# Expert weights of the first quad: per-expert rows of 4 KB for the later half of k, and one give-back for their four slots

## The chip, the core and the metric

The kernel runs on one core of a Trainium2 chip. The metric is the device time of one execution in microseconds, the median of the runs shown. TensorE (PE) multiplies matrices, VectorE (DVE) and ScalarE (ACT) work elementwise, GpSimd (POOL) does a few odd jobs, and SyncE (SP) issues nearly all DMA transfers: it waits on semaphores and puts one transfer after another on a hardware queue, which 16 DMA engines work off in order.

## What is computed

Two layers of a decoder trunk for 256 tokens of width 1024. Each layer has a token mixer (a wide projection, three branches, an output projection) and then a hierarchical mixture of experts. Only the expert part is touched:

```python
def hier_moe(h, w_rg, w_re, w_gate, w_up, w_down):
    ...
    hg = jnp.einsum("nd,edf->nef", t, w_gate)      # 32 experts, d = 1024, f = 256
    hu = jnp.einsum("nd,edf->nef", t, w_up)
    a = jax.nn.silu(hg) * hu * combine[..., None].astype(t.dtype)
    return jnp.einsum("nef,efd->nd", a, w_down).reshape(b, s, d)
```

Every expert has three matrices of 1 MB in float32 (gate, up, down), so a layer reads 96 MB of expert weights.

## The kernel before

**Tiling.** The 32 experts of a layer are taken in eight quads of four. For a quad, PE gathers the chosen tokens (up to 32 for each expert), multiplies them with gate and up, ACT and DVE make the activation, PE multiplies with down and scatters the result back. The contraction over d is cut into eight steps, k = 0 to 7. A row of a weight matrix in memory, seen from one partition p, holds all eight k of that partition one after another: 8 x 256 floats, 8 KB.

**The ring of weight slots.** Weights arrive in slots of 2048 floats for each partition, 1 MB. A quad needs 12 slots (`QUAD_LOADS`): eight for gate and up, four for down. `pos` numbers the 96 loads of a layer in order; `places(pos)` gives the slot, and 20 slots (`RING_E`) are used in turn, so the load at `pos` goes where `pos - 20` was. Pos 0 and pos 11 have places of their own.

**The first quad** is split by k, so that its slots come free step by step. `FIRST_CHUNKS` says which chunk each of pos 0 to 7 holds: a chunk is one pair of k (`part`, 0 to 3) for one pair of experts (`pair`, 0 or 1), both gate and up. `load_expert` (L482) issues two transfers of 512 KB for it (L489), each of 128 partitions x 2 experts x 512 floats, that is rows of 2 KB. All other expert weights go by L498: one transfer of 1 MB in rows of 8 KB.

**When the loads are issued.** The first 20 loads go out while the token mixer before is still running, in the order of `load_ahead`, as its buffers come free: pos 2 and 3, then pos 4, 5 and 9, pos 6 and 10, pos 8, pos 7, pos 0, 14, 15, pos 1, 18, 19, 20, 12, 16, then 13, 17 and 11. PE waits for the weights of pos 4 to 7 by one group semaphore before the third k pair (`wait_weights(pe, 2 * i, routed)` where i is even).

**When slots are given back.** `quads_sp` (L1981) walks on from pos 21 in strict order. Each load waits until PE has read the slot it will overwrite:

```python
if 0 < pos - RING_E < 6:
    sp.wait_ge(R.gu_part, FIRST_CHUNKS[i] // 2 + 1)
elif pos > RING_E and i < 8:
    sp.wait_ge(R.gu_ready, n + 1)
elif pos > RING_E:
    sp.wait_ge(R.y_ready, 2 * (n + 1))
```

`first_quad` (L2092) runs `gather_pair(i)` and `gate_up_pair(i)` for i = 0 to 3. The first three raise `gu_part`, the fourth raises `gu_ready`. So pos 21 and 22 (down weights of quad 1, experts 1 and 2) go out after the first pair, pos 23 (down, expert 3) after the second, pos 24 and 25 (gate and up of quad 2, expert 0) after the third, pos 26 and 27 (gate and up of quad 2, expert 1) after the fourth. Pos 28 to 30 wait for the end of the first quad's down products (`y_ready`), pos 32 and on for the second quad's gate and up.

The weight lines of PE are L2087 (gate and up, first quad), L2142 (gate and up, quads 1 to 6), L2216 (down) and L2116 (gather).

Of the kernel before, what the change touches and what calls it, by code (L numbers as in the profile page):

```python
# [24 lines left out]
P = 128  # L25
# [20 lines left out]
GROUPS, PER_GROUP, F = 4, 8, 256  # L46
# [32 lines left out]
def trunk_program(nc, x, positions, norm1_g, w_in, b_in, attn_sinks, sgu_ln_g, sgu_ln_b, w_spatial,  # L79
# [4 lines left out]
    TB, KB = S // P, D // P  # L84
    assert TB == 2 and KB == 8 and D_IN == ZG + 3 * D

    with ExitStack() as whole:
# [38 lines left out]
        RING_T, RING_A, RING_E = 4, 12, 20  # L126
# [100 lines left out]
        def places(pos, n=1, routed=False):  # L227

            if pos == HELD and not routed:
                return xs[:].rearrange("p t d -> p (t d)").rearrange("p (s n) -> p s n", s=1)  # L230
            if pos == 0:
                return first_slot[:].rearrange("p (s n) -> p s n", s=1)
            s = PLACES[(pos - 2) % RING_E]
            return arena_slots[:, s:s + n, :] if s < RING_A else rest_slots[:, s - RING_A:s - RING_A + n, :]
# [236 lines left out]

        PART = 2 * F
        SPLIT_LOADS = 8
        FIRST_CHUNKS = (2, 0, 1, 3, 4, 5, 6, 7)

        def first_parts(slot):

            return slot.rearrange("p (e a n) -> p e a n", e=2, a=2)

        LAST_DOWN = LAYER_LOADS - 2  # L480

        def load_expert(sp, l, pos, done, routed=False):  # L482

            slot = places(pos, routed=routed)[:, 0, :]
            if pos < SPLIT_LOADS:
                part, pair = divmod(FIRST_CHUNKS[pos], 2)
                for to, w in enumerate((w_expert_gate, w_expert_up)):
                    src = w[l, 2 * pair:2 * pair + 2].rearrange("e (p k) f -> p e (k f)", p=P)
                    sp.dma_start(first_parts(slot)[:, :, to, :], src[:, :, part * PART:(part + 1) * PART]).then_inc(done, 16)  # L489
                return  # L490
            n, i = divmod(pos, QUAD_LOADS)
            if i < 8 and n == QUADS - 1:
                w, e = (w_expert_gate, w_expert_up)[i // 4], i % 4
            elif i < 8:
                w, e = (w_expert_gate, w_expert_up)[i % 2], i // 2
            else:
                w, e = w_expert_down, i - 8
            sp.dma_start(slot, w[l, 4 * n + e].rearrange("(p k) f -> p (k f)", p=P)).then_inc(done, 16)  # L498
# [139 lines left out]
        def trunk_stage(l):  # L638
            with ExitStack():
# [75 lines left out]
                with ExitStack():  # L715
                    @block.sync
                    def _(sp):
# [54 lines left out]
                        def load_ahead(*slots):  # L772
                            for slot in slots:
                                at = PLACES.index(slot) + 2 if slot != PLACES[-1] else 1
                                at += RING_E if at == HELD else 0
                                load_expert(sp, l, at, arrival(False, at))
# [46 lines left out]
                        load_ahead(3, 7)  # L823
                        sp.wait_ge(merged, 4)
                        load_expert(sp, l, 0, arrival(False, 0))
                        sp.wait_ge(quarter_ready, 12)
                        load_ahead(14, 15)
# [967 lines left out]
        def expert_stage(l):  # L1795
# [4 lines left out]
            def wait_weights(eng, pos, routed):  # L1800

                if routed:
                    eng.wait_ge(again_in[pos % RING_E // 4], landed(0, pos, True))
                else:
                    eng.wait_ge(expert_in[pos % RING_E // 4], landed(l, pos))
                    if pos // 4 in (HELD // 4, (HELD + RING_E) // 4):
                        eng.wait_ge(last_up_in, 48 * (l + 1))
                if pos in SINGLE:
                    eng.wait_ge(arrival(routed, pos), (1 if routed else l + 1) * (16 if pos else 32))
# [163 lines left out]
            def load(sp, pos, routed):  # L1973
                if pos > LAST_DOWN and not routed:
                    return
                if pos > LAST_DOWN - 4 and not routed:
                    load_last_down(sp, l, pos - (LAST_DOWN - 3))
                else:
                    load_expert(sp, l, pos, arrival(routed, pos), routed)

            def quads_sp(sp, R, first, last, routed):  # L1981
                for pos in range(first, last):
                    if pos == HELD + RING_E and not routed:
                        continue
                    n, i = divmod(pos - RING_E, QUAD_LOADS)
                    if 0 < pos - RING_E < 6:
                        sp.wait_ge(R.gu_part, FIRST_CHUNKS[i] // 2 + 1)
                    elif pos > RING_E and i < 8:
                        sp.wait_ge(R.gu_ready, n + 1)
                    elif pos > RING_E:  # L1990
                        sp.wait_ge(R.y_ready, 2 * (n + 1))
                    load(sp, pos, routed)
# [74 lines left out]
            def quads_pe(pe, R, a, b, routed):  # L2067
# [8 lines left out]
                def gate_up_pair(i):  # L2076

                    if i % 2 == 0:
                        wait_weights(pe, 2 * i, routed)
                    for k in (2 * i, 2 * i + 1):  # L2080
                        if k < FIRST_DVE:
                            pe.wait_ge(R.first_dve, k + 1)
                        else:
                            pe.wait_ge(R.first_act, k - FIRST_DVE + 1)
                        for e in range(4):
                            w = first_parts(places(FIRST_CHUNKS.index(2 * i + e // 2))[:, 0, :])[:, e % 2, :, (k % 2) * F:(k % 2 + 1) * F]
                            mm = pe.matmul(ps[e * EC:(e + 1) * EC, 0, :].rearrange("p (a f) -> p a f", a=2),  # L2087
                                           xsel[:, k, e * EC:(e + 1) * EC], w, start=(k == 0), stop=(k == KB - 1),
                                           skip_group_check=True)
                    mm.then_inc(R.gu_part if i < 3 else R.gu_ready, 1)  # L2090
# [335 lines left out]
            def extra_rounds_sp(sp, ahead, at):  # L2426

                with seldom(sp, "sp", ahead) as n_extra:
                    for pos in range(at - RING_E, at, 4):
                        wait_weights(sp, pos, False)  # L2430
                    with sp.Fori(0, n_extra):
                        sp.wait_ge(arrive_a, 3)
                        for s in (ex_ranges[(l + 1) % 2], again_range, arrive_a, go_b, go_c):
                            sp.sem_clear(s)
                        sp.sem_inc(go_a, 1)
                        quads_sp(sp, O, 0, LAYER_LOADS, True)
                        sp.wait_ge(arrive_b, 3)
                        for s in (ex_ranges[(l + 1) % 2], again_range, arrive_b, go_a):
                            sp.sem_clear(s)
                        sp.sem_inc(go_b, 1)  # L2440
                    sp.wait_ge(arrive_c, 3)
                    sp.sem_clear(arrive_c)
                    for pos in range(at - RING_E, at):
                        load_expert(sp, l, pos, reload_in)
                    sp.wait_ge(reload_in, 16 * RING_E)
                    sp.sem_clear(reload_in)
                    sp.sem_inc(go_c, 1)

            @block.sync
            def _(sp):  # L2450
                ahead = sp.mark_branch_hint_location()
                sp.wait_ge(quarter_ready, 18)
                for i in range(RING_E):
                    if PLACES[i] in (13, 17):
                        load(sp, i + 2, False)
                sp.wait_ge(logits_ready, 1)
                sp.wait_ge(squares, 2)
                sp.wait_ge(x_copied, 1)
                load(sp, HELD, False)
                at = CUT * QUAD_LOADS + RING_E  # L2460
                sp.sem_inc(mid, 1)
                quads_sp(sp, E, RING_E + 1, at, False)
                sp.wait_ge(cleared, l + 1)
                extra_rounds_sp(sp, ahead, at)
                quads_sp(sp, E, at, LAYER_LOADS, False)
                if not hands_over:
                    sp.dma_start(gf, norm_f_g.partition_broadcast(P)).then_inc(final_in, 16)
# [147 lines left out]
```

## Time and profile before

| | us |
|---|---|
| three timed runs | 1018.99, 1019.67, 1020.12 |
| median | 1019.67 |
| span of the profiled execution, first to last instruction | 1018.6 |
| PE busy, and its share of the span | 957.3 (94%) |
| main DMA queue, share of 16 engines over the span | 79.6% |

The profiled execution's time outside its span is not listed; the median stands 1.07 us above the span. The page cuts the span in 40 slices of 25.5 us. DMA traffic has two long stretches near its highest rate, in slices 11 to 20 and 31 to 39; slices 13 to 20 and 33 to 39 are the expert stages of the two layers, where it is mostly about 425 GB/s. Layer 1 repeats layer 0 with a shift of some 501.8 us. In the granted clock of TensorE nearly all slices stand at full speed.

### The profile page before, as it was taken

To read this page: it belongs to the slowest core of one execution; us is meant where nothing else is said; L and a number is where in the kernel's file an instruction comes from. 1 tells how busy PE (TensorE), PEld (TensorE's weight loads), DVE (VectorE), ACT (ScalarE), POOL (GpSimd) and SP (SyncE) were. 2 spreads that over 40 slices of the span, in tenths; PEclk is the share of its full clock that TensorE was granted. 3 is DMA by queue.
4 is the path that set the end of the run, shared out by engine and by line. 5 is a ranking of instruction groups with operands and counts; after the bars stand their busy time and mean duration, and the time that the engine had idled before them with its cause. 6 is when DMAs were issued, how large, how long until landed. Compare 5 with 4: busy or idle time off the path is not lost.

```text
span 1018.6 us, 15602 instructions
## 1 busy us (share of the span) xinstructions
PE 957.3 (94%) x5898; PEld 666.4 (65%) x5898; DVE 561.1 (55%) x1328; ACT 431.8 (42%) x920; POOL 58.6 (6%) x74
## 2 busy tenths in 40 slices
PE   9999999999999995987999999999999999978876
PEld 7888877778886441533588888777878954334333
DVE  7666788786883332211276668787869633222212
ACT  5434666766444110210354355676764441111122
POOL 1120400000010000000004004000000100000000
PEclk9999999999999999989999999999999999999999
DMA  9975643247999999999997755332589999999996
GB/s 348 349 244 190 196 134 125 83 127 268 409 361 418 425 427 425 425 426 427 418 399 245 233 185 186 124 124 83 172 304 383 386 425 424 425 424 425 427 428 264
DMA packets 97114, 313.03 MB, mean 307 GB/s; under 512 B 13424, under 2 KB 18576, under 8 KB 74512
## 3 DMA queue, kind: packets, MB, share of 16 engines
q1 hardware_dynamic: 96704, 312.04, 79.6%
q8 instruction: 44, 0.72, 0.3%
q14 instruction: 30, 0.25, 0.1%
q10 hardware_dynamic: 336, 0.02, 0.0%
HBM read 310.20 MB, written 1.84 MB: 306 GB/s over the span
## 4 chain that ended last, share of the span: by engine, by line
PE 76%; DMA 13%; SPq 7%; DVE 2%; ACT 1%; issue 1%; POOL 0%; DVEq 0%; POOLq 0%
PE ps L1478 16%; PE ps L1479 15%; PE ps L1480 15%; SPq L498 6%; PE ps L2142 6%; DMA arena<-in_w_expert_up_dram 5%; DMA arena<-in_w_expert_gate_dram 3%; DMA ring_rest<-in_w_expert_up_dram 3%; DMA ring_rest<-in_w_expert_down_dram 3%; PE ps L2116 2%; PE ps L1601 2%; PE ps L1503 2%; PE ps L2216 2%; PE ps L1613 2%; PE ps L2228 2%; PE ps L2087 1%
## 5 line engine op out<-in xcount | busy, mean ns | idle before, releaser
L1130 DVE TENSOR_TENSOR split_w<-arena,split_w 128x512 fp32r<-128x512 f32 (+1 forms) x352 | 233.1, 701 | 101.7 <-ACT split_w L923 98.3
L1478 PE MATMUL ps<-split_w,split_a 128*128 128x512 f32 (+1 forms) x736 | 284.3, 386 | 0.1
L1480 PE MATMUL ps<-split_w,split_a 128*128 128x512 f32 (+1 forms) x736 | 277.0, 376 | 0.0
L1479 PE MATMUL ps<-split_w,split_a 128*128 128x512 f32 (+1 forms) x736 | 276.9, 376 | 0.0
L923 ACT CAST split_w<-arena 128x1024 fp32r<-128x1024 f32 (+1 forms) x171 | 176.2, 1033 | 177.2 <-PE ps L1480 170.3
L1478 PEld LDWEIGHTS ps<-split_w,split_a 128*128 128x128 f32 x736 | 138.5, 188 | 27.9 <-issue 3.4
L1480 PEld LDWEIGHTS ps<-split_w,split_a 128*128 128x128 f32 x736 | 138.4, 188 | 25.9
L1479 PEld LDWEIGHTS ps<-split_w,split_a 128*128 128x128 f32 x736 | 138.7, 188 | 23.2
L2373 DVE SCALAR_TENSOR_TENSOR acts<-ps,wslot,acts 128x256 f32<-128x256 f32 x16 | 7.7, 484 | 168.6 <-ACT acts L2043 145.3
L2142 PE MATMUL ps<-arena,rows 128*32 128x512 f32 x416 | 92.0, 631 | 8.0 <-DMA arena<-in_w_expert_up_dram 4.6
L2142 PE MATMUL ps<-ring_rest,rows 128*32 128x512 f32 x352 | 77.9, 639 | 9.2 <-DMA arena<-in_w_expert_up_dram 9.2
L2043 ACT ACTIVATE acts<-ps,rslot 128x256 f32<-128x256 f32 x16 | 7.6, 474 | 151.0 <-PE ps L2142 146.2
L2116 PEld LDWEIGHTS ps<-arena,work 128*128 128x128 f32 x448 | 52.7, 196 | 28.7 <-issue 24.6
L2116 PE MATMUL ps<-arena,work 128*128 128x128 f32 x448 | 55.6, 283 | 15.5 <-issue 8.8
L2228 PE MATMUL ps<-rows,st 128*128 128x512 f32 x112 | 55.3, 617 | 0.9 <-DVE xs L2354 0.7
L1006 ACT ACTIVATE probs<-probs,neg 128x128 f32<-128x128 f32 x112 | 49.7, 447 | 10.5 <-DVE neg L1254 10.5
L2216 PE MATMUL ps<-arena,acts 128*32 128x512 f32 x272 | 46.3, 639 | 6.1 <-ACT acts L2047 4.2
L1149 DVE SCALAR_TENSOR_TENSOR arena<-ps,rstd,arena 128x512 f32<-128x512 f32 (+2 forms) x68 | 47.2, 730 | 3.9 <-PE ps L1480 3.7
L2142 PEld LDWEIGHTS ps<-arena,rows 128*32 128x32 f32 x416 | 24.1, 116 | 37.6 <-issue 37.6
L2142 PEld LDWEIGHTS ps<-ring_rest,rows 128*32 128x32 f32 x352 | 20.0, 117 | 38.4 <-issue 38.3
L2357 DVE TENSOR_TENSOR xs<-ps,xs 128x512 f32<-128x512 f32 x48 | 33.2, 692 | 18.2 <-PE ps L2228 18.2
L2390 DVE COPY rows<-ps 128x512 f32<-128x512 f32 x14 | 9.7, 692 | 54.3 <-PE ps L2216 54.3
(284 smaller groups left out, 1084.3 us busy)
## 6 DMA issues: line engine op xcount, KB each, us to landing
arena<-in_w_in_dram SPq DMA_DIRECT2D x62, 1024.0 KB, 5.3
arena<-in_w_expert_down_dram SPq DMA_DIRECT2D x36, 1024.0 KB, 19.8
arena<-in_w_expert_gate_dram SPq DMA_DIRECT2D x34, 1024.0 KB, 24.5
arena<-in_w_expert_up_dram SPq DMA_DIRECT2D x32, 1024.0 KB, 24.2
ring_rest<-in_w_expert_down_dram SPq DMA_DIRECT2D x24, 1024.0 KB, 18.2
ring_rest<-in_w_expert_gate_dram SPq DMA_DIRECT2D x22, 1024.0 KB, 24.2
ring_rest<-in_w_expert_up_dram SPq DMA_DIRECT2D x22, 1024.0 KB, 25.9
arena<-in_w_proj_a_dram SPq DMA_DIRECT2D x8, 1024.0 KB, 4.9
```

The lines of the kernel that those rows point to most:

```text
L498: sp.dma_start(slot, w[l, 4 * n + e].rearrange("(p k) f -> p (k f)", p=P)).then_inc(done, 16)
L923: act.copy(whi[:, jj % 2, 0:2 * w], half_slot(jj, w)).then_inc(hi_ready, 1)
L1006: act.activation(probs[:, i, n, lo:hi], probs[:, i, n, lo:hi], ACT.Exp, bias=neg[:, i, tb, n:n + 1], accum_out=den[:, i, tb, n:n + 1])
L1130: dve.tensor_tensor(wlo[:, jj % 2, cols], half_slot(jj, w)[:, cols], whi[:, jj % 2, cols].bitcast(F32), ALU.subtract).then_inc(low_split i ...
L1149: dve.scalar_tensor_tensor(out=z[:, tb, cols], in0=ps[:, bank + tb, 0:w], scalar=rstd[:, tb:tb + 1], in1=z[:, 0, cols], op0=ALU.mult, op1= ...
L1478: pe.matmul(o, hi, rhs_hi, start=first, stop=False)
L1479: pe.matmul(o, hi, rhs_lo, start=False, stop=False)
L1480: return pe.matmul(o, lo, rhs_hi, start=False, stop=last)
L2116: mm = pe.matmul(ps[:, 4 + k // 4, (k % 4) * QUAD:(k % 4 + 1) * QUAD], work[:, tb, k * P:(k + 1) * P], onehot[:, n % 2, tb, :], start=(tb ...
L2142: mm = pe.matmul(ps[e * EC:(e + 1) * EC, n % 2, :].rearrange("p (a f) -> p a f", a=2), xsel[:, k, e * EC:(e + 1) * EC], w, start=(k == 0), ...
L2216: mm = pe.matmul(ps[e * EC:(e + 1) * EC, 2 + nh, :], at_sb[:, kf, e * EC:(e + 1) * EC], w, start=(kf == 0), stop=(kf == 1), skip_group_che ...
L2228: pe.matmul(ps[:, 4 + tb, :], st[:, n % 2, tb * P:(tb + 1) * P], y[:, nh * BANK:(nh + 1) * BANK], start=True, stop=True).then_inc(R.back_r ...
```

## The change

For pos 4 to 7, which before held the k pairs 2 and 3 as chunks of two experts, each slot now holds one expert: `pos - 4`. The slot has gate for k = 4 to 7 in its first half and up for k = 4 to 7 in its second. Each half is one transfer of 512 KB in rows of 4 KB (128 partitions x 1024 floats). The number of transfers, their bytes, their order on the queue and the semaphores that they raise stay. PE reads the same numbers from the new places: gate and up of one k lie 1024 floats apart where they lay 512 apart. Since each of the four slots is now read in both the third and the fourth k pair, all four are given back by `gu_ready`: pos 24 and 25 wait for the fourth pair instead of the third. Pos 21 to 23 keep their waits, and pos 26 and 27 too.

```diff
-        FIRST_CHUNKS = (2, 0, 1, 3, 4, 5, 6, 7)
+        FIRST_CHUNKS = (2, 0, 1, 3)
...
+        def late_parts(slot):
+
+            return slot.rearrange("p (a n) -> p a n", a=2)
...
             slot = places(pos, routed=routed)[:, 0, :]
+            if SPLIT_LOADS // 2 <= pos < SPLIT_LOADS:
+                for to, w in enumerate((w_expert_gate, w_expert_up)):
+                    src = w[l, pos - SPLIT_LOADS // 2].rearrange("(p k) f -> p (k f)", p=P)
+                    sp.dma_start(late_parts(slot)[:, to, :], src[:, KB // 2 * F:KB * F]).then_inc(done, 16)
+                return
...
-                    if 0 < pos - RING_E < 6:
+                    if 0 < pos - RING_E < SPLIT_LOADS // 2:
                         sp.wait_ge(R.gu_part, FIRST_CHUNKS[i] // 2 + 1)
...
-                            w = first_parts(places(FIRST_CHUNKS.index(2 * i + e // 2))[:, 0, :])[:, e % 2, :, (k % 2) * F:(k % 2 + 1) * F]
+                            if i < 2:
+                                w = first_parts(places(FIRST_CHUNKS.index(2 * i + e // 2))[:, 0, :])[:, e % 2, :, (k % 2) * F:(k % 2 + 1) * F]
+                            else:
+                                w = late_parts(places(SPLIT_LOADS // 2 + e)[:, 0, :])[:, :, (k - 4) * F:(k - 3) * F]
```

On SP's queue, where layer 0's pos 4, 5 and 9 are loaded ahead between two loads of the token mixer's `w_proj_b`, stood before:

```order
L790 DMA arena<-in_w_proj_b_dram 128x4x512 [waits low_split]
L489 DMA arena<-in_w_expert_gate_dram 128x2x512 [waits o_lo,obt_ready]
L489 DMA arena<-in_w_expert_up_dram 128x2x512
L489 DMA arena<-in_w_expert_gate_dram 128x2x512
L489 DMA arena<-in_w_expert_up_dram 128x2x512
L498 DMA arena<-in_w_expert_down_dram 128x2048
```

And with the change, whose lines are numbered 9 higher from here on (L799 is the L790 of before, L507 the L498):

```order
L799 DMA arena<-in_w_proj_b_dram 128x4x512 [waits low_split]
L492 DMA arena<-in_w_expert_gate_dram 128x1024 [waits o_lo,obt_ready]
L492 DMA arena<-in_w_expert_up_dram 128x1024
L492 DMA arena<-in_w_expert_gate_dram 128x1024
L492 DMA arena<-in_w_expert_up_dram 128x1024
L507 DMA arena<-in_w_expert_down_dram 128x2048
```

The places in the order and the waits are the same; only the shape of the four transfers differs.

On SP's queue again, in layer 0's expert stage, pos 11 and then pos 21 to 28 stood before as follows (`gu_part0`, `gu_ready0` and `y_ready0` are the three semaphores named above, of layer 0):

```order
L498 DMA xs<-in_w_expert_down_dram 128x2048 [waits x_copied,squares,logits_ready]
L498 DMA arena<-in_w_expert_down_dram 128x2048 [waits gu_part0]
L498 DMA ring_rest<-in_w_expert_down_dram 128x2048 [waits gu_part0] x2
L498 DMA arena<-in_w_expert_gate_dram 128x2048 [waits gu_part0]
L498 DMA arena<-in_w_expert_up_dram 128x2048 [waits gu_part0]
L498 DMA arena<-in_w_expert_gate_dram 128x2048 [waits gu_ready0]
L498 DMA arena<-in_w_expert_up_dram 128x2048 [waits gu_ready0]
L498 DMA arena<-in_w_expert_gate_dram 128x2048 [waits y_ready0]
```

With the change:

```order
L507 DMA xs<-in_w_expert_down_dram 128x2048 [waits x_copied,squares,logits_ready]
L507 DMA arena<-in_w_expert_down_dram 128x2048 [waits gu_part0]
L507 DMA ring_rest<-in_w_expert_down_dram 128x2048 [waits gu_part0] x2
L507 DMA arena<-in_w_expert_gate_dram 128x2048 [waits gu_ready0]
L507 DMA arena<-in_w_expert_up_dram 128x2048 [waits gu_ready0]
L507 DMA arena<-in_w_expert_gate_dram 128x2048 [waits gu_ready0]
L507 DMA arena<-in_w_expert_up_dram 128x2048 [waits gu_ready0]
L507 DMA arena<-in_w_expert_gate_dram 128x2048 [waits y_ready0]
```

Nothing moved in the order; pos 24 and 25 changed the semaphore that they wait for. No instruction of PE, DVE, ACT or POOL is added or moved.

## Rows read from the trace of the kernel before

**Rows 1.** The page's slices: GB/s that the DMA engines moved.

```profile
GB/s 348 349 244 190 196 134 125 83 127 268 409 361 418 425 427 425 425 426 427 418 399 245 233 185 186 124 124 83 172 304 383 386 425 424 425 424 425 427 428 264
```

**Rows 2.** The chain of waits that ended last, in order of time: start, length, what.

```profile
316.62 1.16 PE ps L2072 x8
...
324.00 1.92 PE ps L2087 x16
...
329.43 1.98 PE ps L2116 x16
...
338.30 7.00 PE ps L2142 x64
...
389.20 1.03 SPq L498
...
461.16 27.16 DMA arena<-in_w_expert_gate_dram
...
980.66 26.49 DMA ring_rest<-in_w_expert_down_dram
```

**Rows 3.** Expert stage, layer 0: window; length, PE, PEld, DVE, ACT, POOL, PEclk, DMA, GB/s.

```profile
306.00:346.00 40.00, 39.17 (x315) 23.48 (x315) 12.01 (x68) 14.55 (x41) 2.17 (x2) 1.00 1.01 424
...
466.00:500.00 34.00, 28.70 (x275) 13.92 (x276) 4.98 (x10) 7.62 (x24) 0.00 (x0) 0.95 1.01 425
```

**Rows 4.** Windows in which 2 KB rows of the first quad arrive, columns as before.

```profile
253.00:254.00 1.00, 1.00 (x6) 0.84 (x5) 0.11 (x1) 1.00 (x2) 0.00 (x0) 1.00 1.05 408
254.00:255.00 1.00, 1.00 (x6) 0.84 (x5) 1.00 (x2) 1.00 (x3) 0.00 (x0) 1.00 1.07 404
```

**Rows 5.** DMA issues at 249.99 (pos 4) and 281.25 (pos 7): last, us to landing.

```profile
arena<-in_w_expert_gate_dram SPq DMA_DIRECT2D x1, 512.0 KB, 6.1
...
arena<-in_w_expert_gate_dram SPq DMA_DIRECT2D x1, 512.0 KB, 7.3
```

**Rows 6.** Windows of 1 us after these loads, columns as in rows 3.

```profile
301.00:302.00 1.00, 1.00 (x11) 1.00 (x10) 0.75 (x3) 0.26 (x1) 0.00 (x0) 1.00 0.56 215
302.00:303.00 1.00, 1.00 (x11) 1.00 (x10) 0.28 (x2) 1.00 (x2) 0.00 (x0) 1.00 0.75 182
303.00:304.00 1.00, 1.00 (x11) 1.00 (x10) 1.00 (x2) 0.91 (x3) 0.00 (x0) 1.00 0.88 371
```

**Rows 7.** SP's waits, whole span: line, waited for, us in total, times, longest.

```profile
SPq L498 <- DVE split_w L1127: 20.5, 4, 7.6
```

**Rows 8.** Longest wait for PE of ACT or DVE, 240 to 318 us, columns as before.

```profile
ACT split_w L923 <- PE ps L1480: 22.7, 15, 1.9
```

**Rows 9.** SP's queue over time: start, length, engine, line, transfer.

```profile
301.13 0.34 SPq L498 DMA_DIRECT2D arena<-in_w_expert_gate_dram  x1
...
322.87 0.33 SPq L498 DMA_DIRECT2D ring_rest<-in_w_expert_down_dram  x1
...
325.98 0.33 SPq L498 DMA_DIRECT2D arena<-in_w_expert_gate_dram  x1
...
329.49 0.33 SPq L498 DMA_DIRECT2D arena<-in_w_expert_gate_dram  x1
...
824.71 0.33 SPq L498 DMA_DIRECT2D ring_rest<-in_w_expert_down_dram  x1
...
831.33 0.33 SPq L498 DMA_DIRECT2D arena<-in_w_expert_gate_dram  x1
```

**Rows 10.** DMA issues at 322.87, 325.98 and 824.71: last column us to landing.

```profile
ring_rest<-in_w_expert_down_dram SPq DMA_DIRECT2D x1, 1024.0 KB, 9.6
...
arena<-in_w_expert_gate_dram SPq DMA_DIRECT2D x1, 1024.0 KB, 8.9
...
ring_rest<-in_w_expert_down_dram SPq DMA_DIRECT2D x1, 1024.0 KB, 9.4
```

**Rows 11.** DMA issues at 301.13 and 805.98, onto a nearly empty queue.

```profile
arena<-in_w_expert_gate_dram SPq DMA_DIRECT2D x1, 1024.0 KB, 5.1
...
arena<-in_w_expert_up_dram SPq DMA_DIRECT2D x1, 1024.0 KB, 4.7
```

## The prediction

> **What bounds the kernel now.** I read the slices of the page first. Twice, for some 180 to 200 us, the DMA engines move about 425 GB/s, more than anywhere else: the expert stages [rows 1]. Then the chain of waits. In layer 0 it runs on PE through the first quad (L2072 from 316.62, L2087, and from 329.43 L2116), and from about 389 it is SP's queue and the transfers themselves, the last of them 27.16 us long [rows 2]; layer 1 ends in the same way with a transfer of 26.49 us. The windows settle which of the two it is: from 306 to 346, where the chain names PE, the 16 DMA engines are already busy for a share of 1.01 at 424 GB/s, and in the last stretch, 466 to 500, still 1.01 at 425 [rows 3]. So the queue fills at about 306 and does not run empty before the stage ends. PE is on the chain in that first part only because its reads set when SP may issue. The end of a layer's expert stage is the start of that full queue, plus its bytes at about 424 GB/s, plus any time in which the queue runs dry. The change leaves the bytes of this stretch as they are. It can move the time in two ways only: by what it does to the start of the stretch at 306, or by a hole in it.
>
> **Before the stretch: rows of 4 KB.** Four slots in each layer, 4.19 MB, arrive in longer rows. The nearest price for 2 KB rows is where pos 4 and 5 arrive, 404 to 408 GB/s [rows 4]; where all rows have 8 KB it is 424 [rows 3]. Rows of 4 KB are not in these views, so their rate is bounded by the two: 4.19 MB take 10.4 us at 404 and 9.9 us at 424, so the change saves between 0 and 0.5 us of queue time for each layer, 1.0 us in both. I take about half of it as saved on the queue and nothing of it as saved in the end, for two reasons. First, the loads of pos 4 and pos 7, the first and the last of the four, are issued at 249.99 and 281.25 and their gate halves land 6.1 and 7.3 us later [rows 5], so all of this is over by about 290. Behind them the queue runs empty: the share falls to 0.56, 0.75 and 0.88 in the three windows from 301 to 304 [rows 6], 0.81 us of idle engines together. The next transfer goes out at 301.13 [rows 9], and what SP waits for there is DVE's split of the token mixer's weights, 20.5 us in four waits over both layers [rows 7], not the queue. A queue that is done earlier only idles longer there. Second, in this stretch no compute engine waits for a transfer: the longest wait of ACT or DVE is ACT's for PE, 22.7 us [rows 8], and the three windows show PE busy for the full microsecond [rows 6]. If that cover were gone, the gain would be 1.0 us at most.
>
> **PE's reads.** The third and fourth pair keep their 32 instructions of L2087; 16 take 1.92 us [rows 2], 0.12 us each. The only difference is the distance between gate and up in the slot, 4 KB where it was 2 KB. At L2142 the two lie a whole slot apart, 8 KB, and 64 instructions take 7.00 us [rows 2], 0.11 us each. A larger distance does not cost more there, and a smaller one gains nothing, so I price this at 0 from both sides.
>
> **The later give-back.** This is the term that counts. Before, SP issues pos 24 at 325.98, with pos 25 right behind it, after the third pair, and pos 26 at 329.49, after the fourth [rows 9]. With the change SP stands at pos 24 until the fourth pair is read (L2116 follows it on PE at 329.43 [rows 2]), so pos 24 goes out at 329.49 and pos 25 to 27 behind it, some 0.4 us apart. Queued behind the waiting instruction on SP are pos 25, 26 and 27 alone; the next one, pos 28, waits for the first quad's down products, which come later than this. Nobody waits for these weights soon: they belong to quad 2, which PE reaches after quad 1. So the delay of 3.5 us costs only if the queue runs dry.
>
> What is left on the queue at 329.49 is the end of pos 23. It was issued at 322.87 and landed 9.6 us later, at 332.47 [rows 9, 10]. The margin from the new issue to that landing is 332.47 - 329.49 = 2.98 us. In layer 1 pos 23 was issued at 824.71 and landed 9.4 us later, at 834.11; the issue is at 831.33, margin 2.78 us [rows 9, 10]. Against this stands the time that a transfer on a nearly empty queue needs besides moving its bytes, in front of its first byte and behind its last together. Four such issues, two in each layer, took between 5.1 and 4.7 us to land [rows 11]. One MB alone takes 2.47 us at 424 GB/s [rows 3]. That leaves 2.2 to 2.6 us. How it is divided between front and back doesn't matter: the hole is the overhead less the margin, between 2.2 - 2.98 = -0.8 and 2.6 - 2.78 = -0.2 us, in other words no hole, with little to spare.
>
> The other bound is the one empty queue that the trace shows. There the issue at 301.13 came late, and the engines lost 0.81 us of a full share [rows 6], since they don't finish their parts at the same moment and an early one idles while a late one works. If the same happened at 331 us, it would cost up to 0.8 us for each layer. I take 0.1 us for each, nearer to the first bound, because the late engines set when a load is complete and these are the ones that still have work; I keep 0 and 0.8 for the range. A gain is excluded here: a later issue cannot make the queue fuller.
>
> The Trainium skill has a price for this too: its page "DMA: Bandwidth & Descriptors", in the section "Anatomy of one DMA — SWDGE (gpsimd) path", puts the fixed part of a transfer at about 2.0 us, most of it behind the last byte. That is a fit for another issuing path than SP's; the rows above give 2.2 to 2.6 us here. By its figure the spare time would be an estimated 0.8 to 1.0 us and a hole could be struck out altogether: the sum would stay at 1019.7, where the rows make it 1019.9.
>
> **The sum.** Rows of 4 KB: 0 (bounds -1.0 to 0). PE's reads: 0. Later issue: +0.2 (bounds 0 to +1.6). The profiled span of 1018.6 becomes 1018.8; with the 1.07 us between it and the median of the runs, 1019.67 becomes 1019.9.
>
> **The rivals.**
> *The queue runs dry* at about 331 and 833 us, slower. The late engines and the early ones are so far apart, or the start of a transfer takes so long, that the engines lose what they lost from 301 to 304. For it: a spare time of 0.2 us is small beside 0.81 us of loss seen on one empty queue. Against it: the margins of 2.98 and 2.78 us are longer than every overhead in the rows. Price 0.8 us in each layer, 1.6 us together: 1021.3. Every later transfer is shifted by the hole, since the queue is full from there to the end. It is beyond 0.2% only where the hole is over 1.0 us in each layer.
> *The longer rows come through*, faster. If the queue between 281 and 301 set when the loads from 301 on start, the saved 0.5 us of each layer would be kept: 1018.7. For it: the engines are fully busy before 301. Against it: they are partly idle from 301 to 304, and the issue at 301.13 waits for the split of the mixer's weights.
> *Nothing of this, but another build of the program* with shifts of its own that no row shows: either sign, about as wide as the three runs lie apart, 1.1 us, and rarely twice that.
>
> **How the numbers follow.** A measurement of this kernel can tell about 0.2%, 2 us, from no change; the three runs lie 1.1 us apart. Forecast 0.64, the dry queue 0.22, the longer rows 0.08, the rest 0.06. Nearly all of them stay within 2 us. Slower by more needs a hole of over 1.0 us in each layer, a quarter of the dry queue's chance, and a share of the rest: 0.08. Faster by more needs more than all that the rows could give: 0.04. Same 0.88. The range goes from 1018.5, the longer rows with all their bound and a little of the runs' spread, to 1021.3, the dry queue.
>
> **What the profile after would show.** SP's queue has pos 24 to 27 in one row of issues at about 329.5, and 831.3, directly after the fourth pair. If I am right, pos 24 lands where it did, at 325.98 + 8.9 = 334.88 [rows 9, 10], some 2.5 us after pos 23, and the windows of 1 us from 329 to 333 keep a DMA share near 1. If the queue runs dry, these windows fall to 0.8 or lower, pos 24 lands at 335.5 or later, and all later landings and the end of the stage shift by the same. If the longer rows count, the idle stretch at 301 does not grow, and the first quad begins before 316.62. L2087's 16 instructions stay at 1.9 us. I would be wrong altogether if the transfers of the later stage ran at another rate than 424 to 428 GB/s, or if PE waited for pos 4 to 7 before the third pair, which no row of before shows.

## The result

The changed kernel takes 1022.07 us, the median of ten runs, against 1019.80 us for ten runs of the kernel before. The ratio is 1.0020 with a 95% interval of 1.0012 to 1.0028, so the change costs 2.0 us (1.2 to 2.9). The forecast was 1019.9, in a range up to 1021.3; the forecast is wrong, and of its rivals the one that ran the queue dry (1021.3) came nearest. One execution further down, of the kernel held to ACT's copies, took 1084.48 us at a granted clock of 0.845 where the others have about 0.98, and is left out of that kernel's ratio.

**Where the time went.** SP's queue after the change, in order of time: start, length, line, transfer.

```profile
319.79 0.33 SPq L507 DMA_DIRECT2D arena<-in_w_expert_down_dram  x1
320.17 2.98 SPq L507 DMA_DIRECT2D ring_rest<-in_w_expert_down_dram  x2
329.45 0.33 SPq L507 DMA_DIRECT2D arena<-in_w_expert_gate_dram  x1
329.82 0.43 SPq L507 DMA_DIRECT2D arena<-in_w_expert_up_dram  x1
330.30 0.43 SPq L507 DMA_DIRECT2D arena<-in_w_expert_gate_dram  x1
330.77 0.74 SPq L507 DMA_DIRECT2D arena<-in_w_expert_up_dram  x1
```

Pos 24 to 27 go out in a row from 329.45, as the change says; the last issue before them, pos 23, ended at 323.15 (320.17 + 2.98). For 6.3 us nothing new was queued. The windows of 1 us around this place show what the queue made of it; the last two columns are the DMA engines' busy share and the GB/s that they moved:

```profile
328.00:329.00 1.00, 1.00 (x16) 0.18 (x8) 0.00 (x0) 0.89 (x6) 0.00 (x0) 1.00 1.02 418
329.00:330.00 1.00, 1.00 (x10) 0.68 (x7) 0.00 (x0) 0.99 (x2) 0.00 (x0) 1.00 0.99 418
330.00:331.00 1.00, 1.00 (x12) 1.00 (x11) 0.59 (x2) 0.37 (x1) 0.00 (x0) 1.00 0.82 246
331.00:332.00 1.00, 0.60 (x6) 0.41 (x4) 0.29 (x2) 0.36 (x2) 0.00 (x0) 1.00 0.67 270
332.00:333.00 1.00, 0.94 (x12) 0.34 (x16) 0.00 (x0) 1.00 (x5) 0.00 (x0) 1.00 1.00 410
```

Before, the two middle windows were full:

```profile
330.00:331.00 1.00, 1.00 (x11) 1.00 (x10) 0.55 (x2) 0.42 (x1) 0.00 (x0) 1.00 1.01 426
331.00:332.00 1.00, 0.65 (x6) 0.46 (x4) 0.34 (x2) 0.31 (x2) 0.00 (x0) 1.00 0.97 410
```

From 330 to 332 the engines moved 246 and 270 GB/s instead of 424: (178 + 154) / 424 = 0.78 us of traffic is missing. Layer 1 has the same hole:

```profile
834.00:835.00 1.00, 1.00 (x11) 1.00 (x11) 0.30 (x1) 0.66 (x2) 0.00 (x0) 1.00 1.26 361
835.00:836.00 1.00, 0.90 (x8) 0.71 (x7) 0.59 (x3) 0.06 (x1) 0.00 (x0) 1.00 0.59 147
836.00:837.00 1.00, 0.64 (x8) 0.29 (x12) 0.00 (x0) 1.00 (x5) 0.00 (x0) 1.00 1.08 459
```

For comparing kernels I use one window of 12 us around the place in each layer, since it does not matter there where the windows of 1 us cut. What is missing is 12 x (424 - GB/s) / 424. The changed kernel, layer 0 and layer 1:

```profile
326.00:338.00 12.00, 11.54 (x102) 7.26 (x101) 1.78 (x5) 5.41 (x16) 0.00 (x0) 1.00 0.97 397
...
828.00:840.00 12.00, 11.44 (x99) 5.65 (x97) 0.88 (x3) 5.89 (x18) 0.00 (x0) 1.00 1.00 399
```

The kernel before:

```profile
326.00:338.00 12.00, 11.54 (x101) 7.26 (x101) 1.73 (x5) 5.42 (x16) 0.00 (x0) 1.00 1.01 425
...
828.00:840.00 12.00, 11.54 (x102) 7.26 (x100) 1.90 (x6) 5.42 (x16) 0.00 (x0) 1.00 1.02 429
```

Missing before: nothing. Missing after: 0.76 and 0.71 us, 1.47 us together. Windows of 12 us without a hole differ by some GB/s (in the kernel before 425, 421 and 425 from 326 to 362, and 429, 419 and 427 from 828 to 864), so a single hole is good to about 0.1 us. The stage around them is as it was: of the two windows that answer to [rows 3], the first falls from 424 to 416 GB/s, which is this hole (40 x 8 / 424 = 0.75 us), and the second, 425 before, is at 426.

```profile
306.00:346.00 40.00, 39.18 (x315) 23.44 (x315) 12.04 (x68) 14.48 (x41) 2.17 (x2) 1.00 1.00 416
466.00:500.00 34.00, 28.69 (x258) 13.23 (x262) 4.97 (x10) 7.60 (x24) 0.00 (x0) 0.90 1.01 426
```

**What one pair of traces does not show.** The size of the effect cannot be read from two profiled executions. From the issue of pos 21 in layer 0 to that in layer 1 it is 501.84 us before (319.84 to 821.68) and 504.30 us after (319.79 to 824.09), 2.46 us more, of which the hole of layer 0 is 0.76. The same distance is 503.59 us in the run below that holds pos 25 alone and has no hole, 502.46 us in the second trace of the changed kernel, and 502.44 us with the waits alone, whose profiled execution has both holes and yet the span of the kernel before, 1018.6. So a part of one to two microseconds comes and goes with the execution between the layers; what causes it is not shown. The size is taken from the medians.

**What did not move.** PE reads the new places, in the third and the fourth pair, as fast as the old: 16 instructions take 1.92 us in the third pair, as in [rows 2]. The first quad starts when it did (316.57, in [rows 2] 316.62). The chain of waits after the change, the start of the first quad and the third pair:

```profile
316.57 1.16 PE ps L2081 x8
...
323.96 1.92 PE ps L2099 x16
```

The longer rows come a little faster, 422 and 434 GB/s where [rows 4] has 408 and 404 (other transfers run beside them in both), and it leads to nothing: the queue that is nearly empty from 301 to 303 only becomes emptier.

```profile
253.00:254.00 1.00, 1.00 (x6) 0.84 (x5) 0.15 (x1) 1.00 (x2) 0.00 (x0) 1.00 1.06 422
254.00:255.00 1.00, 1.00 (x6) 0.81 (x5) 1.00 (x2) 1.00 (x3) 0.00 (x0) 1.00 1.06 434
```

```profile
301.00:302.00 1.00, 1.00 (x12) 1.00 (x11) 0.74 (x3) 0.30 (x1) 0.00 (x0) 1.00 0.43 166
302.00:303.00 1.00, 1.00 (x11) 1.00 (x10) 0.29 (x2) 1.00 (x2) 0.00 (x0) 1.00 0.90 154
```

### The profile page after: what moved, and what is told of

Its sections match the earlier page's. It is cut to its first block, busy times and chain, and to the rows that moved or that the text cites. A ratio compares the mean times of both kernels' runs of the same rounds, so it can differ in the third digit from the quotient of the medians.

```text
span 1021.0 us, 15602 instructions
## 1 busy us (share of the span) xinstructions
PE 959.1 (94%) x5898; PEld 669.2 (66%) x5898; DVE 560.6 (55%) x1328; ACT 431.2 (42%) x920; POOL 57.9 (6%) x74
## 4 chain that ended last, share of the span: by engine, by line
PE 79%; DMA 10%; SPq 6%; DVE 2%; ACT 1%; issue 1%; DVEq 0%; POOL 0%; POOLq 0%; ACTq 0%
PE ps L1487 16%; PE ps L1489 15%; PE ps L1488 15%; PE ps L2154 7%; SPq L507 6%; DMA arena<-in_w_expert_up_dram 5%; PE ps L2128 3%; DMA arena<-in_w_expert_gate_dram 3%; DMA ring_rest<-in_w_expert_down_dram 3%; PE ps L2228 2%; PE ps L2240 2%; PE ps L1610 2%; PE ps L1622 2%; PE ps L1512 2%; PE ps L2099 1%; PE ps L1638 1%
## 5 line engine op out<-in xcount | busy, mean ns | idle before, releaser
L2128 PEld LDWEIGHTS ps<-arena,work 128*128 128x128 f32 x448 | 55.8, 206 | 28.4 <-issue 24.3
L2128 PE MATMUL ps<-arena,work 128*128 128x128 f32 x448 | 58.7, 293 | 15.2 <-issue 8.4
L2228 PE MATMUL ps<-arena,acts 128*32 128x512 f32 x272 | 43.6, 595 | 4.6 <-ACT acts L2056 4.6
L2240 PEld LDWEIGHTS ps<-rows,st 128*128 128x128 f32 x112 | 17.7, 189 | 30.5 <-issue 30.5
```

What stands on the lines that cost most here:

```text
L2128: mm = pe.matmul(ps[:, 4 + k // 4, (k % 4) * QUAD:(k % 4 + 1) * QUAD], work[:, tb, k * P:(k + 1) * P], onehot[:, n % 2, tb, :], start=(tb ...
L2228: mm = pe.matmul(ps[e * EC:(e + 1) * EC, 2 + nh, :], at_sb[:, kf, e * EC:(e + 1) * EC], w, start=(kf == 0), stop=(kf == 1), skip_group_che ...
L2240: pe.matmul(ps[:, 4 + tb, :], st[:, n % 2, tb * P:(tb + 1) * P], y[:, nh * BANK:(nh + 1) * BANK], start=True, stop=True).then_inc(R.back_r ...
```

## The experiments

The theory after the two traces: the later issue of pos 24 and 25 lets the queue run dry for about 0.75 us in each layer, and since the queue is full from there to the end of the stage, the end moves by that. The rival: the new rows and places cost the time, or each late issue does, whether the queue runs dry or not. Ten kernels were run in three groups. Each group shared a chip and runs of the kernel before (medians 1020.02, 1019.99 and 1019.92). Edits are to the kernel before where nothing else is said.

### The new waits alone

```diff
-                    if 0 < pos - RING_E < 6:
+                    if 0 < pos - RING_E < 4:
```

> The kernel before with the new waits alone: pos 24 and 25 wait for the fourth k pair, the loads keep their rows of 2 KB. Theory of the hole: the queue runs dry at about 331 us and again in layer 1, as after the change, the windows from 330 to 332 lose some 0.75 us of traffic, and the time is that of the changed kernel, 1021.3 to 1022.3. Rival, the rows of 4 KB or the new places in the slots cost the time: this kernel stays at 1019.8 and the windows stay near 424 GB/s.

Measured: 1022.13 us, ratio 1.0020 (1.0010 to 1.0029). The 12 us windows moved 396 and 399 GB/s, 0.79 and 0.71 us missing:

```profile
326.00:338.00 12.00, 11.54 (x103) 7.14 (x106) 2.22 (x7) 5.56 (x17) 0.00 (x0) 1.00 1.00 396
...
828.00:840.00 12.00, 11.54 (x101) 7.26 (x102) 1.77 (x5) 5.41 (x16) 0.00 (x0) 1.00 0.99 399
```

The old rows of 2 KB and the old places, with the new waits, cost what the whole change costs. The rival of rows and places falls.

### The changed kernel again

No edit to the changed kernel.

> The changed kernel itself, unchanged, on the same chip as the others, for the comparison and for a second trace: 1021.5 to 1022.5. Theory of the hole: windows from 330 to 332 lose 0.7 to 0.8 us of traffic again, and the same in layer 1; what the time has lost beyond 1.5 us is in the last loads of a layer or at the start of layer 1 and differs from one execution to the next.

Measured: 1022.09 us beside the 1022.13 of the waits alone on the same chip; ratio 1.0017 (1.0008 to 1.0026). Windows of 12 us: 395 and 397 GB/s, 0.82 and 0.76 us missing. The hole repeats; rows of 4 KB and their places are worth nothing that can be measured, either way.

### One of the two loads held

```diff
-                    if 0 < pos - RING_E < 6:
+                    if 0 < pos - RING_E < 5:
```

> The kernel before, with pos 25 alone waiting for the fourth pair; pos 24 goes out at 326 as before. Theory of the hole: pos 24 gives the queue 2.47 us more of work, over three times the missing 0.75 us, so no hole is left and the time is that of the kernel before, 1019.8 within 0.6. Rival, any later issue on SP costs by its delay: 3.5 us are held for one load instead of two, and half of the loss, 1.0 us, stays: 1020.9.

Measured: 1020.06 us, ratio 1.0001 (0.9992 to 1.0011). Windows: 423 and 427 GB/s, nothing missing. Pos 25 alone is as late as in the changed kernel, and no cost is seen: pos 24 carries the queue over. The interval, -0.8 to 1.1 us, still holds the 0.9 us of the rival, so the time alone does not rule it out; the trace without a hole speaks against it.

### Layer 0 alone, layer 1 alone

```diff
-                    if 0 < pos - RING_E < 6:
+                    if 0 < pos - RING_E < (4 if l == 0 else 6):
```

> The kernel before, with pos 24 and 25 waiting for the fourth pair in layer 0 alone. Theory of the hole: 0.8 us of traffic lost in layer 0 and none in layer 1, half of the loss of both: 1020.8 to 1021.1. Rival, the loss comes from the passage to layer 1 or from the last loads of layer 1 more than from the two holes: all 2.1 us or none, 1022.1 or 1020.0.

> The kernel before, with pos 24 and 25 waiting for the fourth pair in layer 1 alone. Theory of the hole: 0.75 us of traffic lost in layer 1, none in layer 0, and as much at the end: 1020.6 to 1021.0, as with layer 0 alone. Rival, a hole in layer 1 is worth more than one in layer 0, since nothing follows it that could hide a part: 1021.5.

The second is the same edit with `l == 1`. Measured: 1020.25 us, ratio 1.0005 (0.9995 to 1.0014), and 1020.47 us, ratio 1.0004 (0.9996 to 1.0013). The holes are where they were made, 397 and 428 GB/s in the first (0.76 us and none), 428 and 401 in the second (none and 0.65 us):

```profile
326.00:338.00 12.00, 11.54 (x103) 7.07 (x105) 2.29 (x7) 5.63 (x17) 0.00 (x0) 1.00 1.00 397
828.00:840.00 12.00, 11.54 (x102) 6.68 (x95) 1.58 (x4) 5.41 (x16) 0.00 (x0) 1.00 1.01 428
```

Both medians lie below their ranges (1020.8 to 1021.1, 1020.6 to 1021.0). Each of the two times is compatible with its hole (0.5 and 0.4 us measured, both within -0.5 to 1.4) but not told apart from no change. Neither layer carries the whole 2 us alone, as the first rival would need of one of them, and 1.6 us for layer 1 alone is above its interval. The two do not add up to the 2.0 us of both (0.9 us); the intervals allow it.

### More of the hole

Pos 24 and 25 wait for ACT's activation of the first quad:

```diff
+                    if 4 <= pos - RING_E < 6:
+                        sp.wait_ge(R.silu_done, 1)
-                    if 0 < pos - RING_E < 6:
+                    elif 0 < pos - RING_E < 6:
```

> The kernel before, with pos 24 and 25 waiting for ACT's activation of the first quad, at about 330.4 instead of 329.5 for the fourth pair. Theory of the hole: 0.95 us more than with the fourth pair, so 1.75 us of traffic lost in each layer, 3.5 in both: 1023.5. Rival, the loss does not grow with the delay: 1022.1.

Pos 23 is held too:

```diff
-                    if 0 < pos - RING_E < 6:
+                    if 0 < pos - RING_E < 3:
```

> The kernel before, with pos 23 too waiting for the fourth pair, so that pos 23 to 27 are given back together. Theory of the hole: the queue loses one more transfer of cover, 2.47 us, so 0.8 + 2.5 = 3.3 us of traffic are lost at about 330 us in each layer, and the whole of it reaches the end: 1020.0 + 6.6 = 1026.6, within 1. Rival, a loss of about 2 us that comes once the queue is nearly empty and does not grow with the hole: 1022 to 1023.

Measured: 1023.46 us, ratio 1.0031 (1.0019 to 1.0044), and 1025.30 us, ratio 1.0053 (1.0039 to 1.0066). Their windows of 12 us, first the activation's, then those of three loads held:

```profile
326.00:338.00 12.00, 11.54 (x103) 7.25 (x102) 1.97 (x6) 5.41 (x16) 0.00 (x0) 1.00 0.91 368
828.00:840.00 12.00, 11.54 (x101) 6.29 (x94) 1.58 (x4) 5.41 (x16) 0.00 (x0) 1.00 0.91 363
```

```profile
326.00:338.00 12.00, 11.54 (x102) 7.01 (x104) 2.35 (x7) 5.68 (x18) 0.00 (x0) 1.00 0.79 317
828.00:840.00 12.00, 11.44 (x98) 5.70 (x98) 0.89 (x3) 5.84 (x18) 0.00 (x0) 1.00 0.80 318
```

Missing: 1.58 + 1.73 = 3.3 us, measured 3.2 (1.9 to 4.5); 3.03 + 3.00 = 6.0 us, measured 5.4 (4.0 to 6.7). The loss grows with the hole, nearly one for one. The first time is as forecast (1023.5), though its interval still holds a fixed loss of 2.1 us; the second is below its range (1026.6 within 1), and at 4.0 us or more it rules a fixed loss out.

### Less of the hole

Pos 24 and 25 wait for the end of `spread(0)` on PE (issue at 327.37), or for the third pair and ACT's copies after it (issue at 328.53). The diffs are the one above with `R.st_ready`, and with `R.gu_part` at 3 and then `R.st_evac`.

> The kernel before, with pos 24 and 25 waiting for the end of spread(0), at about 327.6, that is 1.6 us later than before and 1.9 us earlier than with the fourth pair. Theory of the hole: the queue still holds pos 23 and part of pos 22 for some 3 us of work, longer than a new transfer needs to start, so nothing is lost: 1020.0, within 0.6. Rival, each us of delay costs: a third to a half of the loss of 2.1 us, 1020.8.

> The kernel before, with pos 24 and 25 waiting for ACT's copies after spread(0), at about 328.6, that is 0.85 us earlier than the fourth pair. If the hole is a straight line in the time of the issue, 0.75 us less 0.85 leaves none, and the time is 1020.0 to 1020.3. If it falls off slowly at the foot, since some of the 16 engines are done with pos 23 well before the others, 0.3 to 0.6 us of traffic are lost in each layer: 1020.7 to 1021.2.

Measured: 1020.19 us, ratio 1.0001 (0.9992 to 1.0010), windows 423 and 425 GB/s; and 1021.06 us, ratio 1.0014 (1.0005 to 1.0022), windows 416 and 427 GB/s. No price of a delay of some 1.5 us is seen (-0.8 to 1.0 us). The second is less clear: its trace has a hole of 0.23 us in layer 0 and none in layer 1, and the time is 1.4 us (0.5 to 2.2) above the kernel before, as the slow foot would have it, with the trace nearer to the straight line. Two of its executions, at 1023.89 and 1024.26 us, make a part of this; the other nine lie between 1020.02 and 1021.82. One execution is profiled and eleven count for the ratio, so holes that come in some executions and not in others would look like this; that was not shown and stays open.

### The give-back half a microsecond earlier

The changed kernel with the fourth pair ahead of `spread(0)` on PE:

```diff
+                    gate_up_pair(3)
                     if not routed:
                         pe.wait_ge(comb_ready, 1)
                     spread(0)
-                    gate_up_pair(3)
```

> The changed kernel with the fourth pair's products ahead of spread(0) on TensorE, so that the four slots are given back some 0.55 us earlier. Theory of the hole: of 0.75 us in each layer some 0.2 stay, the time falls by about 1.1 us against the changed kernel, to 1020.7 to 1021.2. Rival, rows of 4 KB: the time stays at that of the changed kernel, or rises, since the activation of the first quad comes later.

Measured: 1026.18 us, ratio 1.0053 (1.0039 to 1.0066). The theory's 1020.7 to 1021.2 is missed. The time rises because the activation comes later, as the rival says, but it has nothing to do with rows of 4 KB. PE is idle for 1.52 us before the activation's transposes (L2214), where in the changed kernel it goes on at once; the 0.46 us before the down products (L2228) it has there too.

```profile
328.90 2.03 PE L2128 MATMUL ps<-arena,work 128*128 128x128 f32 x16
332.45 0.50 PE L2214 MATMUL ps<-ident,acts 128*128 128x128 f32 x2 [1.52 <-DVE acts L2385]
333.42 1.07 PE L2228 MATMUL ps<-arena,acts 128*32 128x512 f32 x3 [0.46 <-ACT acts L2056]
```

In layer 0 TensorE's clock fell after this idle time: from 334 to 336 the granted clock is 0.50, the lower of its two levels (1.2 GHz), and the group of L2228 above takes 1.07 us, where it takes 0.63 us in the changed kernel. In layer 1 PE is idle for the same 1.52 us, but the clock stays at 1.00 and the group takes 0.63 us. So pos 28, which waits for the down products, follows pos 21 after 19.54 us in layer 0 and 17.90 us in layer 1, against 15.97 us in both layers of the changed kernel. Pos 32 and on are late by it too (348.30, in the changed kernel 345.31), and the queue runs short for a second and a third time:

```profile
326.00:338.00 12.00, 10.01 (x72) 4.57 (x74) 0.88 (x3) 5.40 (x16) 0.00 (x0) 0.86 0.98 399
338.00:350.00 12.00, 12.00 (x98) 5.18 (x90) 2.97 (x7) 1.39 (x7) 0.00 (x0) 1.00 0.97 357
350.00:362.00 12.00, 11.18 (x79) 6.46 (x79) 5.52 (x11) 2.83 (x11) 0.00 (x0) 1.00 0.96 381
...
852.00:864.00 12.00, 11.18 (x75) 4.52 (x68) 5.54 (x8) 1.43 (x3) 0.00 (x0) 1.00 0.99 394
```

Missing in layer 0 are 0.71, 1.90 and 1.22 us; in layer 1, whose first two windows stand at 422 and 421 GB/s, 0.06, 0.08 and 0.85 us. That is 4.8 us, and the time is 5.4 us (4.0 to 6.7) above the kernel before. The first hole, the one that the edit was to close, is about as large as in the changed kernel in layer 0 (0.71 us against 0.76) and nearly gone in layer 1 (0.06 us against 0.71). So the edit does not test cleanly what it was made for, but it shows the same price at other places.

### All of them in one table

Holes are from the 12 us windows of the one profiled execution (three of them for each layer in the last row); the change in time is the ratio less one, times 1020.

| kernel | pos 24 goes out in layer 0 | missing traffic, both layers, us | change in time, us |
|---|---|---|---|
| before | 325.98 | 0.0 | - |
| pos 25 alone held | 326.20 | 0.0 | 0.1 (-0.8 to 1.1) |
| held to `spread(0)` | 327.37 | 0.0 | 0.1 (-0.8 to 1.0) |
| layer 1 alone | 325.36 | 0.7 | 0.4 (-0.4 to 1.3) |
| layer 0 alone | 328.94 | 0.8 | 0.5 (-0.5 to 1.4) |
| held to ACT's copies | 328.53 | 0.2 | 1.4 (0.5 to 2.2) |
| changed | 329.45 | 1.5 | 2.0 (1.2 to 2.9) |
| waits alone | 329.01 | 1.5 | 2.0 (1.0 to 3.0) |
| changed, again | 328.85 | 1.6 | 1.7 (0.8 to 2.7) |
| held to the activation | 330.21 | 3.3 | 3.2 (1.9 to 4.5) |
| pos 23 held too | 329.25 | 6.0 | 5.4 (4.0 to 6.7) |
| changed, fourth pair first | 328.39 | 4.8 | 5.4 (4.0 to 6.7) |

The issue times shift with the start of the first quad, whose pos 21 goes out between 319.20 and 320.06. Counted from pos 21, pos 24 follows after 6.14 us before, 7.77 us when held to `spread(0)`, 8.80 us when held to ACT's copies, 9.65 us with the fourth pair and 10.61 us when held to the activation. Apart from one row, held to ACT's copies, the change in time follows the missing traffic within its interval. No version beats the kernel before: what the longer rows save lies ahead of an empty queue, and the give-back by expert is what costs.

## Why the prediction was wrong, point by point

**What bounds the kernel** was right: the end of a stage is the start of the full queue, its bytes, and its holes. Holes of 1.5, 3.3 and 6.0 us moved the end by 2.0, 3.2 and 5.4.

**Rows of 4 KB, 0 in the end,** was right, and so was the reason; the waits alone give the same time as the whole change. **PE's reads, 0,** right: 1.92 us for 16, as before.

**The later give-back** was the step that failed, a term of +0.2 us (bounds 0 to 1.6) that measured 1.5 us of traffic and 2.0 us (1.2 to 2.9) in time. The issue time was right to 0.04 us in layer 0 (329.49 forecast, 329.45 found); in layer 1 all came 2.4 us later. The mistake is in "the hole is the overhead less the margin". I measured the margin to the landing of pos 23. A landing is one moment, the end of the last part, and the traffic it stands for fades out before it. In the changed kernel pos 23 went out at 322.82 (320.17 + 2.98 - 0.33) and took the first of these rows, pos 24 the second:

```profile
ring_rest<-in_w_expert_down_dram SPq DMA_DIRECT2D x1, 1024.0 KB, 9.4
...
arena<-in_w_expert_gate_dram SPq DMA_DIRECT2D x1, 1024.0 KB, 6.0
```

Pos 23 landed at 332.22, but the traffic was already at 246 GB/s between 330 and 331. And pos 24, with a margin of 332.22 - 329.45 = 2.77 us, needed 6.0 us where the four issues of [rows 11] needed 4.7 to 5.1: an overhead of 6.0 - 2.47 = 3.5 us, not 2.2 to 2.6. In layer 1 the landings would have hidden the hole altogether. Pos 23 went out at 827.13 and pos 24 at 833.75, with

```profile
ring_rest<-in_w_expert_down_dram SPq DMA_DIRECT2D x1, 1024.0 KB, 9.6
...
arena<-in_w_expert_gate_dram SPq DMA_DIRECT2D x1, 1024.0 KB, 5.4
```

so they landed at 836.73 and 839.15, 2.42 us apart, as close as two loads behind one another on a full queue, while the windows from 834 to 836 moved 361 and 147 GB/s. The single packets of the trace show why. In the expert stage there are 16 packets of 4 bytes for each load of 1 MB, by their number one at the end of each engine's part. Of pos 23's in layer 0, 13 stand between 330.37 and 330.53 and the last at 331.81; in layer 1, 14 between 834.54 and 834.95 and the last at 836.34. Most engines are through about 1.8 us before the landing, some 1 us after the issue of pos 24, and pos 24's first packets start only then (330.47 and 834.75). Most of these first packets take 0.7 to 1.3 us for their 8 KB, where a packet on the full queue takes 0.31 us. In layer 1 nearly all of the hole is this slow start (a mean share of 0.93 over 834 to 836, at 254 GB/s); in layer 0 some engines are idle as well (0.82 and 0.67). Why the first packets are slow is not in the trace.

**The other bound**, 0.8 us for each layer from the empty queue at 301, was the right neighbour to look at, and its size was nearly met (0.76 and 0.71). I took a value next to the other end, since the late engines still had work. That reason was wrong: what the early ones lose is not made up while the queue is full to the end. I also read that neighbour by the busy share, 0.81 us of idle engines. By the GB/s of the same [rows 6], 215, 182 and 371, it is (209 + 242 + 53) / 424 = 1.19 us, which would have put the rival at 1019.67 + 2.4 = 1022.1. The share reads too high when the queue is nearly empty: the changed kernel's window from 834 to 835 has a share of 1.26 and moves 361 GB/s.

**The rule of the Trainium skill** on the fixed part of a transfer (page "DMA: Bandwidth & Descriptors", section "Anatomy of one DMA — SWDGE (gpsimd) path", about 2.0 us) would have struck the hole out. The runs speak against using it in this way: 2.8 to 3.0 us between an issue and the landing of what is ahead of it were not enough. They do not speak against the figure itself, which is for another issuing path.

**The rivals.** The dry queue was given 0.22 and is what happened. Its price, 1.6 us, fits the holes (1.47, 1.50 and 1.58 us in three traces); the time is some half a microsecond above it, within the intervals. The longer rows did not come through.

**The chances** rested on a spare time of 0.2 to 0.8 us that was the difference of two numbers of about 2.5, each good to half a microsecond. That is not a basis for 0.64.

## What to carry to other kernels

Where a stage is bound by a full DMA queue, a later issue costs what the queue loses in traffic, and nothing if a whole transfer is still queued behind the one that is running out. Measure that cover in untouched transfers, and a hole in GB/s: here 2.8 to 3.0 us from the issue to the landing of the last load ahead lost 0.65 to 0.82 us of traffic, 3.4 us (fourth pair first, layer 0) 0.71 us, 3.6 to 3.9 us (held to ACT's copies) at most 0.23 us, and 4.7 to 5.0 us (held to `spread(0)`) nothing; with one load more (2.5 us) in the queue no cost of a delay of 3.5 us was seen. Longer rows are worth something only where the queue does not run empty behind them. And one profiled execution against another is no measure of a change of 2 us here, since the executions differ by as much.

## What the runs showed of the hardware

- A queue can lose 0.7 us of traffic with no gap between landings: layer 1's pos 23 and 24 land 2.42 us apart over a hole of 0.71 us.
- From the issue on a nearly empty queue (329.45) to full traffic again (the window from 332) it took about 2.5 us; in the last two of them the engines moved 246 and 270 GB/s.
- The parts of one load end up to 1.8 us apart (834.54 to 836.34), and the first 8 KB packets of a load that meets such a queue took mostly 0.7 to 1.3 us instead of 0.31.
- After the same 1.52 us of idle PE the granted clock fell to 0.50 in layer 0 and stayed at 1.00 in layer 1 (the run with the fourth pair first).
- The busy share of the DMA engines overstates the traffic when a queue starts again: 1.26 at 361 GB/s, and 1.06 at 197 GB/s in the run with the waits alone:

```profile
330.00:331.00 1.00, 1.00 (x11) 0.97 (x9) 0.85 (x3) 0.00 (x0) 0.00 (x0) 1.00 1.06 197
```
